# Two-block transformer kernel, second block's mixer: the norm of the differential heads moved two units later in VectorE's written order

## The chip, the core and the metric

One core of one Trainium2 chip runs the whole program. The metric is the device time of one execution in microseconds (us), the smaller the better; the time given for a kernel is the median over its runs. Two kernels are compared on the same chip.

## The reference, cut to what matters

The program computes two transformer blocks of two layers each over 256 tokens of width 1024, in float32. The change lies in the second block, in its `hybrid_mixer`, which runs once in each of the second block's two layers:

```python
def hybrid_mixer(n, pos, layer_idx, w_in, ...):
    proj = n @ w_in
    ...
    o_a = mla_causal_attention(q_a, k_a, v_a)                        # 6 latent heads, width 64
    o_b = diff_causal_attention(..., dvh, pos, slopes[:6], lam)      # 6 differential heads, width 64
    o_b = rmsnorm(o_b, sub_norm) * (1.0 - lam_init)                  # the norm that is moved
    o_c = moba_causal_attention(...)                                 # 4 block heads, width 64
    o = jnp.concatenate([from_heads(o_a), from_heads(o_b), from_heads(o_c)], axis=-1)
    return o @ w_out
```

After the mixer a layer has a cross attention to 256 memory tokens and a squared-relu feed-forward part.

## The kernel before, in words

The order of the work on each engine is written out by hand: one stream of instructions each for TensorE (PE), VectorE (DVE), ScalarE (ACT), GpSimd (POOL) and SyncE (SP, which issues the weight loads). Each stream runs in order, and the streams meet only in semaphores. Tokens lie on the 128 partitions in two tiles (t = 0, 1). A float32 product is made of three matmuls with rounded high and low parts (lines 937 to 939); ScalarE makes a weight piece's high part, VectorE its low part (`ahead`, line 2270).

The mixer's attention is cut into 12 **units**, here called unit 1 to unit 12 (in the code 0 to 11): 1 to 6 are differential heads, 7 and 8 the block heads, 9 to 12 the latent heads. Odd units are for token tile 0, even ones for tile 1. A unit passes through these steps:

- scores, TensorE (line 1090);
- **mask**, VectorE (`mask`, lines 2423 to 2433): adds the mask and finds each row's maximum;
- exponentials, ScalarE (line 1837);
- transposes of the probabilities, TensorE (line 1102), and their copy out, ScalarE (line 1851);
- **values**, TensorE (line 1145), all into one PSUM bank, so that the values of a unit wait until the unit before has been divided (`pe.wait_ge(o_out, u)`);
- **division**, VectorE (`end`: line 2457 the reciprocal, line 2465 the product, which writes the output rows H and signals `o_out`).

TensorE's order late in the stage is: scores of unit k+1, transposes of unit k-1, values of unit k-2, and so on. Between the transposes of unit 12 and the values of unit 11 stands its **tail**, `mixed` (line 1662): it waits for `rows_ready`, which the norm signals, and then transposes two batches of output heads (line 1009), the second of them the differential heads. Behind it come the values of units 11 and 12, one more batch, and then the output projection, whose first matmuls are at lines 937 to 939.

VectorE's loop in `attention` (line 2403) makes, in step i (counted from 0, units named from 1) for i above 7: the mask of unit i+1 (for i below 12), the division of unit i-2, then `between(i)`. In `between` the norm of the differential heads has two parts. In step 8 the squares, sums and the mean of the differential outputs are made, and POOL is asked for their power -1/2 (line 845). In step 10 VectorE waits for POOL, scales the factors by 1 - lambda (line 3116), and multiplies H by the factor and by the gain for both token tiles (lines 3119 and 3120, twice each): five instructions, the last of which signals `rows_ready`. In step 13, the last, it makes the low parts of the first two transposed batches (`turn_mix`).

Of the kernel before, what the change touches and what calls it, by code (L numbers as in the profile page):

```python
# [117 lines left out]
def build(nc, a, out):  # L118
    ctx = ExitStack()
    with ctx:  # L120
# [245 lines left out]
        def bc4(ap, n):  # L366

            return ap.unsqueeze(2).to_broadcast([ap.shape[0], ap.shape[1], n])
# [1878 lines left out]
        def _(dve):  # L2247
# [4 lines left out]
            def seq(ins):  # L2252

                done[0] += 1
                ins.then_inc(dve_seq, 1)
                dve.wait_ge(dve_seq, done[0])

            def power():

                c.pow += 1  # L2260
                dve.wait_ge(pow_out, c.pow)

            def ahead():

                limit = len(raw_of) if past_moe[0] else before_moe
                while c.split < min(c.piece + AHEAD, limit):
                    i = c.split
                    r, n = raw_of[i], size_of[i]
                    dve.wait_ge(w_hi, i + 1)
                    dve.tensor_tensor(Wl[:, i % SPLITS, 0:n], ring[:, r % RING, 0:n],  # L2270
                                      Wh[:, i % SPLITS, 0:n].bitcast(F32), ALU.subtract).then_inc(w_lo, 1)
                    c.split += 1
# [9 lines left out]
            def turn_mix(batches, batches_hi):  # L2282

                for (_, lo, _), (_, hi, _) in zip(batches, batches_hi):
                    c.mix += 1
                    dve.wait_ge(mix_hi, c.mix)
                    dve.tensor_tensor(lo, PS[:, c.turn % 4, :].rearrange("p (m s) -> p m s", m=2),
                                      hi.bitcast(F32), ALU.subtract).then_inc(turn_out, 1)
                    c.turn += 1
# [7 lines left out]
            def eps_in(n, width):  # L2297

                dve.tensor_scalar(st[:, 0:n], st[:, 0:n], 1.0 / width, EPS, ALU.mult, ALU.add).then_inc(pow_in, 1)
# [103 lines left out]
            def attention(units, extras={}, between=None, early={}, deep=None):  # L2403
# [66 lines left out]
                for i in range(count + 2):  # L2470
                    if i < count:
                        mask(i)
                    if i in early:
                        early[i]()
                    if deep is not None and i > deep + 1:
                        end(i - 3)
                    turned_values = units[0]["end"][0] == "nsa"
                    if turned_values and 1 <= i <= count:
                        weigh(i - 1)
                    if between is not None:  # L2480
                        between(i, count + 2)
                    if not turned_values and i >= 2 and (deep is None or i <= deep):
                        end(i - 2)
# [385 lines left out]
            for layer in range(LAYERS):  # L2869
# [170 lines left out]
                def second_glu():  # L3040

                    c.lin += 1
                    glu(1)

                attention(nsa_units(), nsa_extras, between, {1: second_glu})
                mix_low(1)
                ahead()
# [12 lines left out]
            for layer in range(LAYERS):  # L3060
# [42 lines left out]
                def between(i, n):  # L3103
                    if i in (0, 2, 5):
                        c.piece += 1
                        ahead()
                    elif i == 8:
                        for t in range(T):
                            view = H[:, t, 384:768]
                            seq(dve.tensor_tensor(norm_tmp[:], view, view, ALU.mult))  # L3110
                            seq(dve.tensor_reduce(st[:, 6 * t:6 * t + 6],
                                                  norm_tmp[:].rearrange("p (h d) -> p h d", d=64), AX, ALU.add))
                        eps_in(12, 64)
                    elif i == 10:
                        power()
                        seq(dve.tensor_scalar(rs[:, 0:12], rs[:, 0:12], 1.0 - lam0, None, ALU.mult))
                        for t in range(T):
                            view = H[:, t, 384:768].rearrange("p (h d) -> p h d", d=64)
                            seq(dve.tensor_tensor(view, view, bc4(rs[:, 6 * t:6 * t + 6], 64), ALU.mult))
                            ins = dve.tensor_tensor(view, view, bc[:, b0:b0 + 64].unsqueeze(1).to_broadcast([P, 6, 64]),  # L3120
                                                    ALU.mult)
                        ins.then_inc(rows_ready, 1)
                    elif i == n - 1:
                        turn_mix(t_mixed_lo[0:2], t_mixed[0:2])

                c.turn += len(t_latent(layer)) + len(t_diff)
                attention(mixer_units(layer), mix_extras, between, deep=DEEP)
                c.lin = base + 18
                turn_mix(t_mixed_lo[2:4], t_mixed[2:4])
# [83 lines left out]
```

## Time and profile before

| | |
|---|---|
| median of 3 runs | 2399.97 us (2398.38 to 2402.65) |
| the profiled execution, its own time | 2401.94 us |
| the profiled execution, its span | 2400.2 us |
| busy in the span: TensorE, VectorE, ScalarE, POOL | 2358.4, 1726.8, 1438.9, 69.7 us |
| instructions | 31905 |

The profile is of one execution. Its span is the time from the first to the last instruction; the execution's own time is 1.74 us longer. A row of the timeline gives the start, the length, the engine, the line, the operation, the tile written and the tiles read, and how many instructions were merged into the row; in square brackets stands how long the engine had been idle before, and which engine's work ended that. Starts and lengths overlap a little, since an engine takes up the next instruction before the last has fully ended. "PEclk" is the clock that was granted to TensorE, as a share of full speed.

### The profile page before, as it was taken

What the parts mean: (1) busy time and instruction counts of PE and PEld (TensorE: products, weight loads), DVE (VectorE), ACT (ScalarE), POOL (GpSimd) and SP (SyncE); (2) the same over time, 40 slices, a digit from 0 to 9 for tenths busy, and PEclk for the clock granted to TensorE, in tenths of its full rate; (3) what the DMA queues carried; (4) which work ended last, traced back from release to release, by engine and by line L of the source; (5) the groups of instructions that cost most, each with busy time, mean ns of one, the idle gap of its engine ahead of it and who ended that gap; (6) DMA issues with size and microseconds to landing.
All of it is one profiled execution on the core that took longest, in us unless ns stands there. A gap on an engine that the chain in (4) does not pass through costs nothing.

```text
span 2400.2 us, 31905 instructions
## 1 busy us (share of the span) xinstructions
PE 2358.4 (98%) x12092; PEld 1937.0 (81%) x12092; DVE 1726.8 (72%) x2123; ACT 1438.9 (60%) x1685; POOL 69.7 (3%) x79
## 2 busy tenths in 40 slices
PE   9999999999999999999999999999999999999998
PEld 8688888678888888888888888887788888787887
DVE  8665446759988889898988888767465565755555
ACT  6544445657777777777777777665544445554443
POOL 1000000001000000000000000001000000000000
PEclk9999999999999999999999999999999999999999
DMA  7545555419999999999999999615535542452551
GB/s 264 163 142 191 193 183 163 143 62 331 370 340 379 345 371 339 379 345 378 341 368 349 374 346 372 222 54 211 174 123 180 186 149 84 175 184 97 195 190 44
DMA packets 249704, 569.99 MB, mean 237 GB/s; under 512 B 9664, under 2 KB 20352, under 8 KB 249600
## 3 DMA queue, kind: packets, MB, share of 16 engines
q1 hardware_dynamic: 249456, 568.30, 67.3%
q8 instruction: 70, 1.15, 0.2%
q14 instruction: 34, 0.28, 0.0%
q10 hardware_dynamic: 144, 0.26, 0.0%
HBM read 562.82 MB, written 1.05 MB: 235 GB/s over the span
## 4 chain that ended last, share of the span: by engine, by line
PE 92%; DVE 5%; ACT 1%; issue 1%; POOL 0%; POOLq 0%; ACTq 0%; DVEq 0%
PE PS L937 27%; PE PS L939 26%; PE PS L938 26%; PE PS L1090 2%; PE PS L1564 1%; PE PS L1145 1%; PE PS L1393 1%; PE PS L1102 1%; PE PS L1213 1%; PE PS L1009 1%; PE PS L1128 1%; DVE Wl L2270 1%; PE PS L1034 1%; PE PS L1354 1%; PE PS L998 1%
## 5 line engine op out<-in xcount | busy, mean ns | idle before, releaser
L2706 DVE TENSOR_TENSOR Wl<-ring,Wh 128x2048 fp32r<-128x2048 f32 x334 | 761.9, 2298 | 100.9 <-ACT Wh L1988 100.9
L1988 ACT ACTIVATE Wh<-ring 128x2048 fp32r<-128x2048 f32 x334 | 639.8, 1918 | 127.8 <-PE PS L939 127.8
L2270 DVE TENSOR_TENSOR Wl<-ring,Wh 128x2048 fp32r<-128x2048 f32 (+2 forms) x192 | 431.2, 2251 | 278.0 <-ACT Wh L1743 277.4
L1743 ACT ACTIVATE Wh<-ring 128x2048 fp32r<-128x2048 f32 (+2 forms) x192 | 361.6, 1890 | 237.4 <-PE PS L939 236.6
L937 PE MATMUL PS<-Wh,HTh 128*128 128x512 f32 (+3 forms) x1184 | 465.8, 393 | 4.3 <-DVE Wl L2270 2.4
L939 PE MATMUL PS<-Wh,HTl 128*128 128x512 f32 (+3 forms) x1184 | 457.3, 386 | 0.0
L938 PE MATMUL PS<-Wl,HTh 128*128 128x512 f32 (+3 forms) x1184 | 456.7, 386 | 0.0
L937 PE MATMUL PS<-Wh,xgh 128*128 128x512 f32 x896 | 354.3, 395 | 1.8 <-DVE Wl L2706 1.2
L939 PE MATMUL PS<-Wh,xgl 128*128 128x512 f32 x896 | 349.5, 390 | 0.0
L938 PE MATMUL PS<-Wl,xgh 128*128 128x512 f32 x896 | 348.9, 389 | 0.0
L937 PEld LDWEIGHTS PS<-Wh,HTh 128*128 128x128 f32 x1184 | 223.5, 189 | 50.4 <-issue 4.2
L939 PEld LDWEIGHTS PS<-Wh,HTl 128*128 128x128 f32 x1184 | 223.4, 189 | 43.9
L938 PEld LDWEIGHTS PS<-Wl,HTh 128*128 128x128 f32 x1184 | 223.9, 189 | 41.1
L937 PEld LDWEIGHTS PS<-Wh,xgh 128*128 128x128 f32 x896 | 168.2, 188 | 37.5 <-DVE Wl L2706 2.0
L939 PEld LDWEIGHTS PS<-Wh,xgl 128*128 128x128 f32 x896 | 168.2, 188 | 35.9
L938 PEld LDWEIGHTS PS<-Wl,xgh 128*128 128x128 f32 x896 | 168.4, 188 | 33.5
L937 PE MATMUL PS<-Wh,hmh 128*128 128x512 f32 x448 | 175.9, 393 | 0.7 <-DVE hml L2720 0.7
L939 PE MATMUL PS<-Wh,hml 128*128 128x512 f32 x448 | 174.5, 389 | 0.0
L938 PE MATMUL PS<-Wl,hmh 128*128 128x512 f32 x448 | 174.3, 389 | 0.0
L937 PE MATMUL PS<-Wh,hTh 128*128 128x512 f32 x368 | 143.6, 390 | 0.0
L939 PE MATMUL PS<-Wh,hTl 128*128 128x512 f32 x368 | 143.2, 389 | 0.0
L938 PE MATMUL PS<-Wl,hTh 128*128 128x512 f32 x368 | 143.2, 389 | 0.0
(369 smaller groups left out, 2396.8 us busy)
## 6 DMA issues: line engine op xcount, KB each, us to landing
ring<-in_moe_w_gate SPq DMA_DIRECT2D x112, 1024.0 KB, 7.1
ring<-in_moe_w_up SPq DMA_DIRECT2D x112, 1024.0 KB, 7.3
ring<-in_moe_w_down SPq DMA_DIRECT2D x112, 1024.0 KB, 6.7
ring<-in_mlp_w SPq DMA_DIRECT2D x64, 1024.0 KB, 5.3
ring<-in_w_in SPq DMA_DIRECT2D x27, 1024.0 KB, 5.2
ring<-in_w_out SPq DMA_DIRECT2D x16, 1024.0 KB, 7.1
ring<-in_cross_wkv SPq DMA_DIRECT2D x16, 1024.0 KB, 12.4
ring<-in_ffn_w_gate SPq DMA_DIRECT2D x14, 1024.0 KB, 5.1
```

The source lines that it names most:

```text
L937: pe.matmul(out_, hi, high, start=start, stop=False)
L938: pe.matmul(out_, hi, low, start=False, stop=False)
L939: return pe.matmul(out_, lo, high, start=False, stop=stop)
L998: mm = pe.matmul(PS[:, bank, 0:n], lhs(kc, t), w[:, kc, c0:c0 + n], start=(kc == 0), stop=(kc == k - 1))
L1009: mm = pe.transpose(PS[0:width, c.turn % 4, off:off + rows], s, ident[0:rows, 0:rows])
L1034: mm = pe.transpose(PS[:, 2 * t + half, i * P:i * P + P], src[:, t, kc * P:kc * P + P], ident[:])
L1090: mm = pe.matmul(PS[:, 2 * (u % 2) + at[m] // 2, (at[m] % 2) * S:(at[m] % 2) * S + un["kl"]], q, key, start=(k == 0), stop=(k == len(un["s ...
L1102: mm = pe.transpose(PS[0:size, 4 + x % 2, m * P:m * P + P], un["home"][:, m, kb * P:kb * P + size], ident[:])
L1743: act.activation(Wh[:, i % SPLITS, 0:n], ring[:, r % RING, 0:n], ACT.Copy).then_inc(w_hi, 1)
L1988: act.activation(Wh[:, (base + i) % SPLITS, :], ring[:, (raw + i) % RING, :], ACT.Copy).then_inc(e_hi, 1)
L2270: dve.tensor_tensor(Wl[:, i % SPLITS, 0:n], ring[:, r % RING, 0:n], Wh[:, i % SPLITS, 0:n].bitcast(F32), ALU.subtract).then_inc(w_lo, 1)
L2706: dve.tensor_tensor(Wl[:, (base + i) % SPLITS, :], ring[:, (raw + i) % RING, :], Wh[:, (base + i) % SPLITS, :].bitcast(F32), ALU.subtract) ...
```

## The change

The second part of the norm is emitted in step 12 instead of step 10 of VectorE's loop. It is the same five instructions on the same data, and it applies to both layers. No other engine's order is touched. Step 10 then holds the mask of unit 11 and the division of unit 8; step 11 the mask of unit 12 and the division of unit 9; step 12 the division of unit 10 and then the norm; step 13 the division of unit 11 and `turn_mix`.

```diff
@@ -3111,7 +3111,7 @@
                             seq(dve.tensor_reduce(st[:, 6 * t:6 * t + 6],
                                                   norm_tmp[:].rearrange("p (h d) -> p h d", d=64), AX, ALU.add))
                         eps_in(12, 64)
-                    elif i == 10:
+                    elif i == 12:
                         power()
                         seq(dve.tensor_scalar(rs[:, 0:12], rs[:, 0:12], 1.0 - lam0, None, ALU.mult))
                         for t in range(T):
```

## Rows read from the trace of the kernel before

**Rows 1.** The page: the chain that ended last, by engine.
```profile
PE 92%; DVE 5%; ACT 1%; issue 1%; POOL 0%; POOLq 0%; ACTq 0%; DVEq 0%
```

**Rows 2.** The waits from 1624 to 1640 us (engine, line waited for: total us, times, longest).
```profile
DVE coef L2457 <- PE PS L1145: 4.8, 3, 2.2
...
PE PS L1145 <- DVE H L2465: 2.2, 3, 1.2
```

**Rows 3.** The timeline of VectorE, first of the two mixers (start, length).
```profile
1628.45 0.18 DVE L2457 RECIPROCAL coef<-PS 128x4 f32<-128x4 f32 x1 [1.54 <-PE PS L1145]
...
1629.01 0.16 DVE L3116 TENSOR_SCALAR rs<-rs 128x12 f32<-128x12 f32 x1
...
1630.86 0.56 DVE L3120 TENSOR_TENSOR H<-H,bc 128x384 f32<-128x384 f32 x1
1631.33 0.42 DVE L2423 CUSTOM_DVE_ANT_0 SM<-PS,causal 128x256 f32<-128x256 f32 x1
...
1632.21 0.18 DVE L2457 RECIPROCAL coef<-PS 128x4 f32<-128x4 f32 x1
1632.43 0.42 DVE L2465 TENSOR_TENSOR H<-PS,coef 128x256 f32<-128x256 f32 x1
1635.00 0.18 DVE L2457 RECIPROCAL coef<-PS 128x4 f32<-128x4 f32 x1 [2.15 <-PE PS L1145]
```

**Rows 4.** The timeline of TensorE, the same stretch.
```profile
1628.34 1.33 PE L1090 MATMUL PS<-scr 64*128 64x256 f32 x8
...
1630.54 1.00 PE L1145 MATMUL PS<-scr,PT 128*128 128x65 f32 x8
...
1633.00 1.97 PE L1145 MATMUL PS<-scr,PT 128*128 128x65 f32 x16 [1.23 <-DVE H L2465]
1634.80 0.61 PE L1102 MATMUL PS<-ident,SM 128*128 128x128 f32 x4
1635.25 1.04 PE L1009 MATMUL PS<-ident,H 128*128 128x128 f32 x8
...
1637.36 1.08 PE L1145 MATMUL PS<-scr,PT 128*128 128x65 f32 x8 [0.68 <-DVE H L2465]
...
1638.63 0.47 PE L937 MATMUL PS<-Wh,HTh 128*128 128x512 f32 x1
```

**Rows 5.** The timeline of POOL, the same stretch.
```profile
1624.19 2.26 POOL L845 TENSOR_TENSOR rs<-st,mhalf 128x12 f32<-128x12 f32 x1 [77.04 <-DVE st L2299]
```

**Rows 6.** The timeline of the second mixer: last gain of the norm, two TensorE rows.
```profile
2061.70 0.56 DVE L3120 TENSOR_TENSOR H<-H,bc 128x384 f32<-128x384 f32 x1
...
2063.84 1.97 PE L1145 MATMUL PS<-scr,PT 128*128 128x65 f32 x16 [1.23 <-DVE H L2465]
...
2066.09 1.04 PE L1009 MATMUL PS<-ident,H 128*128 128x128 f32 x8
```

**Rows 7.** Busy time by stretch, behind the first mixer.
```profile
core 0: us, PE busy (x) PEld busy (x) DVE busy (x) ACT busy (x) POOL busy (x), PEclk, DMA share, GB/s
1650.00:1700.00 50.00, 50.00 (x239) 41.73 (x238) 29.34 (x40) 26.28 (x34) 2.67 (x1) 1.00 0.75 259
```

**Rows 8.** The timeline of TensorE in the first block's attention, ahead of a clock fall.
```profile
115.81 0.61 PE L1102 MATMUL PS<-ident,SM 128*15 128x128 f32 x4 [1.52 <-DVE SM L2449]
```

**Rows 9.** Busy time by stretch: first block's attention, and the program's end.
```profile
117.00:118.00 1.00, 1.00 (x7) 1.00 (x8) 0.00 (x0) 0.04 (x1) 0.00 (x0) 0.59 0.05 16
...
2392.00:2396.00 4.00, 0.09 (x1) 0.00 (x0) 3.62 (x10) 1.15 (x1) 1.27 (x2) 1.00 0.32 129
```

**Rows 10.** The timeline of TensorE: a first-block projection (12 matmuls), then the mixer's own.
```profile
501.50 0.76 PE L937 MATMUL PS<-Wh,HTh 128*128 128x512 f32 x1 [0.46 <-DVE scr L3037]
...
506.32 0.40 PE L939 MATMUL PS<-Wh,HTl 128*128 128x512 f32 x1
...
1639.18 0.40 PE L939 MATMUL PS<-Wh,HTl 128*128 128x512 f32 x1
1639.41 0.40 PE L937 MATMUL PS<-Wh,HTh 128*128 128x512 f32 x1
```

## The prediction

> **What bounds the kernel now.** I read the page first. Its chain that ended last is 92% TensorE [rows 1], so the question for any edit is whether TensorE waits longer or shorter for it. I then took the waits around the first mixer's end. There TensorE stands still three times for a division on VectorE, 2.2 us in all, and VectorE in turn stands still three times for TensorE's values, 4.8 us [rows 2]. So the end of the mixer is a ping-pong of two engines, in which neither is full: values of a unit, its division, values of the next. What counts is which instructions of VectorE lie between the two.
>
> The timelines of the two engines give the order. VectorE divides unit 8 at 1628.45, and from 1629.01 to the end of the last gain at 1630.86 + 0.56 = 1631.42 it makes the norm; then come the mask of unit 12 from 1631.33 and the division of unit 9 from 1632.21 to 1632.43 + 0.42 = 1632.85 [rows 3]. TensorE had the values of unit 9 ready at 1630.54 + 1.00 = 1631.54, and waited 1.23 us until 1633.00 to start those of unit 10 [rows 4]. The reader should see that the norm delays this step: without it VectorE would have waited for TensorE at that point. POOL's power is done at 1626.45, long before the norm in either place [rows 5].
>
> The other thing to see is who waits for the norm. TensorE's tail, two batches of transposes at 1635.25, starts while the last transposes of unit 12 run out, with no idle time ahead of it [rows 4]. The norm was done 3.83 us before that. The change spends this slack.
>
> **The change, step by step, in the first mixer.** It takes five VectorE instructions with one signal and one wait for POOL from behind the division of unit 8, and puts them behind the division of unit 10. Nothing is added or removed, and there are no DMAs among them.
>
> Removed ahead of the mask of unit 12. The division of unit 8 to the norm's first instruction takes 1629.01 - 1628.45 = 0.56 us, so the mask could start at 1629.01, but its scores end at 1628.34 + 1.33 = 1629.67 [rows 4]. I take 0.03 us from TensorE's end to VectorE's start, as at 1633.00 + 1.97 to 1635.00 [rows 3, 4]: the mask starts at 1629.70 and ends 1632.21 - 1631.33 = 0.88 later, at 1630.58. VectorE now waits for the values of unit 9 and divides them from 1631.57. The division takes 0.64 us (1632.21 to 1632.85), TensorE's answer 0.15 us (1632.85 to 1633.00). So the values of unit 10 start at 1631.57 + 0.64 + 0.15 = 1632.36, which is **0.64 us earlier** than now. The mask's being early by 1.63 us is worth nothing more, because the transposes of unit 12 stand behind those values on TensorE.
>
> Added ahead of the tail. The values of unit 10 end at 1634.33 instead of 1634.97, and their division starts at 1634.36. The norm follows 0.56 us later, at 1634.92, and takes 1631.42 - 1629.01 = 2.41 us: it signals at 1637.33. The tail starts 0.15 us later, at 1637.48, where it now starts at 1635.25. That is **2.23 us later**. TensorE has the last transposes of unit 12 from 1634.16 to 1634.77 and then nothing: its stream is in order, and behind the waiting tail stand the values of units 11 and 12, which are otherwise ready. This is the new stall, 2.71 us long.
>
> Behind the tail nothing of the order changes. The values of unit 11 follow the tail, their division follows them and waits for nothing else, the values of unit 12 wait for that division as they do now (0.68 us), then the last batch and the projection, now at 1638.63 [rows 4]. ScalarE and the low parts made by VectorE follow the same transposes. All of it shifts by 2.23 us. The memory tokens' load is held until the values of unit 12, and shifts too; its users come later. Behind the mixer TensorE is busy 50.00 of 50 us [rows 7]: there is no wait of TensorE there that could take up the shift.
>
> The second mixer has the same pattern: last gain at 2061.70, values of unit 10 at 2063.84 after the same 1.23 us, tail at 2066.09 [rows 6]. The distances are 2.14 and 4.39 us, against 2.14 and 4.39 in the first. So it costs the same, and the **order alone costs 2 x 2.23 = 4.46 us**.
>
> **What the new gap does to TensorE's clock** is not in this sum, and the trace does not show such a gap at this place, so I bound it. Against any cost stands the program's end, where TensorE was busy for 0.09 of 4.00 us and its granted clock was still 1.00 [rows 9]. For a cost stands the first block's attention: after an idle stretch of 1.52 us at 115.81, with only short matmuls around it, the granted clock went from 1.00 to 0.59 in the microsecond from 117 [rows 8, 9], that is from the upper level of 2.4 GHz to the lower of 1.2 GHz for part of it. Our stage has gaps of 1.23 and 0.68 us now [rows 4]; it would have a gap of 2.71 us with short matmuls on both sides. A price for the fall comes from a projection run while the clock was low: its first 12 matmuls start from 501.50 to 506.32, 0.438 us apart, where the mixer's own projection has 0.23 [rows 10]. The 11 steps lose 11 x 0.21 = 2.3 us. The lower bound of a fall is 0, if it comes in the gap and is over before dense work starts; nothing in the rows makes a gain of it. Of these I take 1.2 us, half of 2.3, because part of the low stretch would pass while TensorE is idle in the gap or in short matmuls that also wait for divisions. I count one fall net of those that already happen: the runs of before lie 4.27 us apart, so they may hold one or two already, while the profiled one has none here.
>
> The Trainium skill ("TensorE: Matmul & The Clock Gate", section "A second HAM failure mode: psum-queue depth-cycling") says that frequent short idle times between groups of matmuls can make the clock swing between its levels, at a loss of throughput. By that rule the time is above the sum of the order alone; the fall at 117 agrees with it, the program's end does not speak for it.
>
> The sum: 4.46 + 1.2 = 5.7 us. Against the profiled execution's own time that is 2401.94 + 5.7 = 2407.6, which lies 1.97 us above the median of the runs; against the median, which I predict, 2399.97 + 5.7 = **2405.6 us**.
>
> **The rivals.**
> *The order alone* (0.35). The clock stays at 1.00 through the gap, as over the idle 4 us at the end. Then it is 2399.97 + 4.46 = 2404.4 us.
> *The clock falls in both mixers and for a full low stretch* (0.08): 4.46 + 2 x 2.3 = 9.1, so 2409.1 us.
> *The shift is taken up later* (0.10). For it: behind the mixer is a cross attention with waits of its own. Against it: those waits are on work that itself hangs on TensorE's order. If half of it is caught, 2402.2 us.
> *Not slower* (0.04). The two-engine ping-pong gains and the tail is not held: this needs the norm to be over before the last transposes of unit 12 end, at 1634.77. Then only the 0.64 us per mixer remains, 2399.97 - 1.3 = 2398.7 us. It would hold if VectorE had the norm's 2.41 us free between 1630.58 and 1634.36. It has idle time there, but the order puts the norm behind a division that starts only at 1634.36, so I see no way but a compiled order that differs from the written one. That the change does nothing is in the same case: the moved rows are on the chain today.
>
> **How the numbers follow.** The forecast, the order's cost and one fall of the clock more than before, has 0.43; its own range is 2404.8 (hardly any price of the fall) to 2408.5. The range for all reaches from 2402.8, under the case of the order alone, to 2409.0; outside it lie the not slower case, most of the case taken up later, and part of the double fall, under 2 in 10 together. About 0.2%, 4.8 us, is what a measurement of this kernel can tell from no change, and that is 2404.8: the order alone falls just under it. Slower by more: 0.43 of the forecast, 0.08, and a third of the 0.35, so 0.62. Faster by more than 0.2% no case gives: 0.01. The rest, 0.37, is within.
>
> **What would show it.** In the profile of the changed kernel the norm's first instruction (line 3116, now at 1629.01) comes some 5.9 us later, right behind a division; VectorE has a new wait of about 1 us for the values of unit 9; TensorE's wait ahead of the values of unit 10 falls from 1.23 to about 0.6 us; and a new wait of TensorE of 2.7 us appears at line 1009, released by H of line 3120, once in each mixer. From the mask of unit 11 to the first projection matmul there must be 2.2 us more at full clock. The granted clock by stretch decides between the forecast and the first rival: below 1.00 between the tail and some microseconds into the projection, or 1.00 throughout. I am wrong if the tail's wait is under 2 us, if TensorE has less idle time than before in the cross attention, or if the two mixers differ in anything but the clock.

## The result, and the profile after

| | kernel before | changed kernel |
|---|---|---|
| median | 2399.51 us (6 runs, 2394.4 to 2403.81) | 2412.64 us (6 runs, 2410.77 to 2413.95) |
| the profiled execution, its own time | 2401.94 us | 2412.96 us |
| its span | 2400.2 us | 2411.2 us |
| its mean granted clock | 0.994 | 0.991 |

The changed kernel is slower by a ratio of 1.0047, with an interval of 1.0035 to 1.0058. The ratio is worth 11.3 us; the medians of six runs each are 13.1 us apart, and the two profiled spans 11.0 us. The prediction has 5.7 us. The sign is right; the time lies 3.6 us above the range. Of the 90 runs of the kernel before that were made beside the experiments below, one, at 3387.45 us and a mean clock of 0.651, is left out throughout.

The page first: the instructions are 31905 as before, and the chain that ended last has the same split as in [rows 1].

```profile
PE 92%; DVE 5%; ACT 1%; issue 1%; POOL 0%; POOLq 0%; ACTq 0%; DVEq 0%
```

The waits from 1622 to 1650 us in the changed kernel (engine, line waited for: total us, times, longest):

```profile
PE PS L1009 <- DVE H L3120: 2.6, 1, 2.6
PE PS L1145 <- DVE H L2465: 1.5, 3, 0.7
```

The first row is new: TensorE's tail (line 1009) waits once, 2.6 us, for the last product of the norm. The last row was 2.2 us with 1.2 as the longest [rows 2]. So one wait became shorter and a new one came. VectorE's timeline in the first mixer says why:

```profile
1628.63 0.42 DVE L2423 CUSTOM_DVE_ANT_0 SM<-PS,causal 128x256 f32<-128x256 f32 x1 [0.63 <-PE PS L1090]
...
1630.49 0.18 DVE L2457 RECIPROCAL coef<-PS 128x4 f32<-128x4 f32 x1 [0.88 <-PE PS L1145]
...
1633.29 0.18 DVE L2457 RECIPROCAL coef<-PS 128x4 f32<-128x4 f32 x1 [2.15 <-PE PS L1145]
...
1633.85 0.17 DVE L3116 TENSOR_SCALAR rs<-rs 128x12 f32<-128x12 f32 x1
...
1635.70 0.56 DVE L3120 TENSOR_TENSOR H<-H,bc 128x384 f32<-128x384 f32 x1
```

The mask of unit 12 now waits 0.63 us for its scores, the division of unit 9 waits 0.88 us for its values, and the norm starts right behind the division of unit 10, at 1633.85. In [rows 3] the same instruction starts at 1629.01. TensorE's timeline, first mixer and then two rows of the second:

```profile
1628.52 1.09 PE L1102 MATMUL PS<-ident,SM_MIX 128*128 128x128 f32 x8
...
1631.28 1.97 PE L1145 MATMUL PS<-scr,PT 128*128 128x65 f32 x16 [0.60 <-DVE H L2465]
...
1636.31 1.97 PE L1009 MATMUL PS<-ident,H 128*128 128x128 f32 x8 [2.62 <-DVE H L3120]
1638.08 0.95 PE L1145 MATMUL PS<-scr,PT 128*128 128x65 f32 x4
1639.71 1.94 PE L1145 MATMUL PS<-scr,PT 128*128 128x65 f32 x8 [0.68 <-DVE H L2465]
1641.45 1.06 PE L1009 MATMUL PS<-ident,H 128*128 128x128 f32 x4
1642.16 0.78 PE L937 MATMUL PS<-Wh,HTh 128*128 128x512 f32 x1
...
1646.49 0.60 PE L1009 MATMUL PS<-ident,H 128*128 128x128 f32 x4
...
2073.33 1.97 PE L1009 MATMUL PS<-ident,H 128*128 128x128 f32 x8 [2.61 <-DVE H L3120]
...
2083.44 0.60 PE L1009 MATMUL PS<-ident,H 128*128 128x128 f32 x4
```

And the rows of the kernel before that these are compared with and that did not stand ahead of the prediction:

```profile
1629.61 1.09 PE L1102 MATMUL PS<-ident,SM_MIX 128*128 128x128 f32 x8
...
1636.12 0.56 PE L1145 MATMUL PS<-scr,PT 128*128 128x65 f32 x4
...
1638.27 0.61 PE L1009 MATMUL PS<-ident,H 128*128 128x128 f32 x4
1641.49 0.60 PE L1009 MATMUL PS<-ident,H 128*128 128x128 f32 x4
```

Read the lengths, not only the gap. The eight transposes of the tail took 1.04 us [rows 4] and now 1.97; the eight matmuls of the values of unit 12 took 1.08 and now 1.94. They are the same instructions at half speed. The windows of the changed kernel (columns as in [rows 7]) show it as the granted clock:

```profile
1630.00:1634.00 4.00, 3.09 (x27) 2.64 (x25) 1.29 (x5) 1.85 (x6) 0.00 (x0) 1.00 0.02 4
1634.00:1638.00 4.00, 1.69 (x8) 1.69 (x9) 2.15 (x5) 0.70 (x2) 0.00 (x0) 0.64 0.00 0
1638.00:1642.00 4.00, 3.32 (x17) 3.16 (x16) 1.93 (x6) 0.66 (x2) 0.00 (x0) 0.50 0.00 0
1642.00:1646.00 4.00, 4.00 (x13) 3.21 (x12) 0.88 (x2) 0.60 (x1) 0.00 (x0) 0.58 0.78 262
...
2068.00:2084.00 16.00, 12.40 (x61) 11.11 (x62) 5.79 (x15) 2.83 (x7) 0.00 (x0) 0.68 0.26 91
```

The clock goes from the upper level, 2.4 GHz (1.00), to the lower, 1.2 GHz (0.50), in the new gap, and stays low into the projection. Time at the lower level is the missing share of a window divided by one half: 0.36 x 4 / 0.5 = 2.9 us, then 4.0, then 0.42 x 4 / 0.5 = 3.4, together 10.2 us. The second mixer gives 0.32 x 16 / 0.5 = 10.2 us as well. In the profiled execution of before the clock is 1.00 in all of these stretches. The fall itself lies inside the gap, in a microsecond in which TensorE does nothing:

```profile
1635.00:1636.00 1.00, 0.00 (x0) 0.00 (x0) 0.97 (x3) 0.00 (x0) 0.00 (x0) 0.55 0.00 0
```

**Where the 11 us come from.** I measure the stage from the eight transposes of SM_MIX to the fourth batch of transposes (line 1009, x4), from start to start. Before it takes 1641.49 - 1629.61 = 11.88 us, after it 1646.49 - 1628.52 = 17.97 us: 6.09 us more. Between the starts of the tail and of the fourth batch nothing differs but the clock: 1641.49 - 1635.25 = 6.24 us before and 1646.49 - 1636.31 = 10.18 us after, so **3.94 us are the clock** and the other **2.15 us are the order** (predicted 2.23). The 3.94 split by starts of successive rows: tail 1.77 against 0.87, values of unit 11 with the wait 1.63 against 1.24, values of unit 12 1.74 against 0.91, last batch 0.71 against 0.36, the twelve projection matmuls 4.33 against 2.86. That is 0.90 + 0.39 + 0.83 + 0.35 + 1.47. More than half of it is in the short matmuls ahead of the projection. The second mixer gives 17.90 against 11.89 us, 6.01 more. The sum of both, 12.1 us, less the 1.09 us by which this execution was ahead when it reached the first mixer (1628.52 against 1629.61), is the 11.0 us of the span.

### The profile page after: what moved, and what is told of

Same layout as the page of the kernel before. It is cut to its first block, busy times and chain, and to the rows that moved or that the text cites. A ratio compares the mean times of both kernels' runs of the same rounds, so it can differ in the third digit from the quotient of the medians.

```text
span 2411.2 us, 31905 instructions
## 1 busy us (share of the span) xinstructions
PE 2365.9 (98%) x12092; PEld 1944.8 (81%) x12092; DVE 1726.5 (72%) x2123; ACT 1438.9 (60%) x1685; POOL 69.7 (3%) x79
## 4 chain that ended last, share of the span: by engine, by line
PE 92%; DVE 5%; ACT 1%; issue 1%; POOL 0%; POOLq 0%; ACTq 0%; DVEq 0%
PE PS L937 26%; PE PS L939 26%; PE PS L938 26%; PE PS L1090 2%; PE PS L1145 1%; PE PS L1564 1%; PE PS L1102 1%; PE PS L1393 1%; PE PS L1009 1%; PE PS L1213 1%; PE PS L1128 1%; DVE Wl L2270 1%; PE PS L1034 1%; PE PS L1354 1%; PE PS L998 1%
```

## The experiments

Two theories stood at this point. The first: the order costs what the prediction says, and all of the rest is the clock, which the gap brings down in both mixers. The rival: the low clock only goes along with a delay of another kind, so that it would stay if the clock did. Beside them stood the question whether the kernel before has falls of its own, which would change what counts as the price.

The kernel before was run again beside each group of kernels. Its medians were 2401.59 us beside e1 to e4, 2401.40 beside e5 to e8, and 2401.83 beside e9 to e12. Where an edit adds lines above, the same instruction stands one or two lines further down in the rows (L3121 or L3122 for L3120).

**e1: the norm one step later instead of two.** It is behind the division of unit 9.

```diff
-                    elif i == 10:
+                    elif i == 11:
```

> The norm's second part one step behind its old place, in step 11, behind the mask of unit 12 and the division of unit 9. Theory (each mixer loses first to the order, then to a fall of TensorE's clock in the new gap): here the norm ends before the last transposes of unit 12 do, so the tail waits for nothing or under 0.2 us, no gap over 1 us is there, the clock stays at 1.00 in both mixers, and each mixer is 0.6 us shorter than before: about 1.3 us off the kernel before, 0.9995 of it. Rival (any norm behind the last mask delays the mixer, because the divisions behind it come late): 1 to 4 us above the kernel before.

Measured: 2398.17 us median, ratio 0.9984 (0.9976 to 0.9993), so faster than before by 3.4 us, more than was expected. TensorE's timeline:

```profile
1629.52 1.09 PE L1102 MATMUL PS<-ident,SM_MIX 128*128 128x128 f32 x8
...
1632.28 1.97 PE L1145 MATMUL PS<-scr,PT 128*128 128x65 f32 x16 [0.60 <-DVE H L2465]
1634.08 0.61 PE L1102 MATMUL PS<-ident,SM 128*128 128x128 f32 x4
1634.53 1.07 PE L1009 MATMUL PS<-ident,H 128*128 128x128 f32 x8
...
1640.81 0.60 PE L1009 MATMUL PS<-ident,H 128*128 128x128 f32 x4
```

The wait ahead of the values of unit 10 is 0.60 us, as in the changed kernel, and the tail has no wait, as in before: it starts while the last transposes of unit 12 run out. The stage takes 11.29 us, 0.59 less than before (0.64 was worked out for this part). This is the gain of the change without its cost. It is 1.2 us for both mixers; the median gained 3.4, and the rest goes with the clock (below).

**e2 and e3: the gap filled, and the same filling in the kernel before.** The kernel has a helper, `unread`, whose 128x512 matmuls write to a PSUM bank that nobody reads. Ten of them go between the last transposes of unit 12 and the tail, the computed result being untouched. e2 is the change with them, e3 the kernel before with them.

```diff
-                def unread(i):
+                def unread(i, count=UNREAD):
...
-                    for k in range(UNREAD):
+                    for k in range(count):
...
+                amid[12, 1] = lambda: unread(12, 10)
```

> The change, and in each mixer ten 128x512 matmuls whose result nobody reads, between the transposes of unit 12 and the tail, where the changed kernel's TensorE stood idle for 2.62 us. Theory: they take 10 x 0.23 = 2.3 us and fit in the gap, the granted clock is 1.00 from 1630 to 1650 us, and only the cost of the order is left: 2 x 2.2 = 4.4 us above the kernel before (ratio 1.0018), some 8 us under the changed kernel. Rival (the loss of 12 us is in the waits themselves, the low clock only accompanies it): 11 to 13 us above the kernel before, as without them.

> The kernel before, with the same ten unread matmuls ahead of the tail in each mixer: TensorE is delayed there by 2.3 us, but busy. Theory: a delay of the tail of the same size as the change's, at full clock, costs its own length and no more: 2 x 2.3 = 4.6 us above the kernel before (1.0019), clock 1.00. Rival (whatever delays the tail costs about 6 us a mixer, since something behind it goes late): 11 to 13 us.

Measured: e2 2403.74 us, 1.0011 (1.0003 to 1.002); e3 2403.88 us, 1.0013 (1.0004 to 1.0022). TensorE's timeline of e2:

```profile
1626.49 1.09 PE L1102 MATMUL PS<-ident,SM_MIX 128*128 128x128 f32 x8
...
1631.42 2.56 PE L1672 MATMUL PS<-HTl 128*128 128x512 f32 x10
1634.28 1.09 PE L1009 MATMUL PS<-ident,H 128*128 128x128 f32 x8 [0.30 <-DVE H L3121]
...
1640.56 0.60 PE L1009 MATMUL PS<-ident,H 128*128 128x128 f32 x4
```

Its windows over both mixers:

```profile
1620.00:1650.00 30.00, 28.15 (x180) 23.69 (x179) 19.52 (x56) 13.20 (x23) 4.93 (x2) 1.00 0.39 142
2050.00:2085.00 35.00, 33.16 (x208) 26.98 (x208) 23.95 (x69) 17.47 (x32) 4.93 (x2) 1.00 0.39 142
```

This is the pair that decides. The ten matmuls are over before the norm is, since the tail still waits 0.30 us for it; so the tail is released by the same work as in the changed kernel, and what differs is the clock: 1.00 in both mixers. Its stage takes 1640.56 - 1626.49 = 14.07 us. Against the changed kernel's 17.97 that is **3.90 us for the clock**, against before's 11.88 it is **2.19 us for the order**. The rival falls, since the delay goes when the clock stays. With the extra work the change is at a ratio of 1.0011 to before, without it at 1.0047: 0.0036, or 8.6 us, are gained by adding work. In e3, where no gap is there to take them in, the same ten matmuls cost 14.17 - 11.88 = 2.29 us per mixer, and the clock is 1.00 too. The 1.23 us ahead of the values of unit 10 are still idle in e3.

**e4: the moved norm in the first of the two mixers only.**

```diff
-                    elif i == 10:
+                    elif i == (12 if layer == 0 else 10):
```

> The change in the first layer's mixer alone. Theory: the two mixers are alike and independent, each costs its order and its own clock fall: about 6 us above the kernel before (1.0025), the clock low from about 1635 to 1645 us and 1.00 in the second mixer. Rival (the first fall makes the second likelier, or the cost is not additive): under 4 or over 9 us.

Measured: 2405.65 us, 1.0015 (1.0006 to 1.0024), so the expected 1.0025 lies just above the interval. Its windows:

```profile
1620.00:1655.00 35.00, 30.84 (x186) 25.62 (x186) 20.53 (x71) 16.14 (x31) 3.98 (x2) 0.85 0.30 109
2050.00:2085.00 35.00, 32.58 (x239) 27.16 (x239) 25.35 (x90) 19.50 (x39) 2.76 (x2) 1.00 0.23 81
```

The clock falls in the mixer that has the gap and not in the one that has not. The missing 0.15 of 35 us is 10.5 us at the lower level, about as long as in the changed kernel. The stage of the first mixer takes 17.84 us, 5.96 more than before; the median is 4.1 more, over runs of before that hold falls of their own (e10, below). The fall in the first mixer did not bring one in the second; this is one execution's trace.

**e5: the kernel before, its own 1.23 us gap filled.** Four of the same matmuls stand in that gap, ahead of the values of unit 10 (`amid[11, 1] = lambda: unread(11, 4)`).

> The kernel before, with four unread 128x512 matmuls in each mixer in its own idle stretch of 1.23 us ahead of the values of unit 10 (4 x 0.23 = 0.9 us, so they delay nothing). Step 11 had come out 3.4 us under the kernel before, where the order explains 1.3. Theory (in some executions of the kernel before the clock falls in its mixers too, though not in the profiled one): the fillers keep it up, and the median is 1 to 3 us under the kernel before, 0.9988 to 0.9996, with fewer executions above 2402 us. Rival (the kernel before has no falls there, and the rest of step 11's gain lies elsewhere): the same as the kernel before within 0.0004.

Measured: 2399.42 us, 0.9992 (0.9982 to 1.0003). It is 2.0 us less by the medians, and the interval takes in no change. It alone does not settle whether the kernel before loses time to its own gap.

**e6: the norm cut in two.** Its scaling and the first token tile are in step 11, the second tile and the signal in step 12.

```diff
-                    elif i == 10:
-                        power()
-                        seq(dve.tensor_scalar(rs[:, 0:12], rs[:, 0:12], 1.0 - lam0, None, ALU.mult))
-                        for t in range(T):
+                    elif i in (11, 12):
+                        if i == 11:
+                            power()
+                            seq(dve.tensor_scalar(rs[:, 0:12], rs[:, 0:12], 1.0 - lam0, None, ALU.mult))
+                        for t in (i - 11,):
...
-                        ins.then_inc(rows_ready, 1)
+                        if i == 12:
+                            ins.then_inc(rows_ready, 1)
```

> The scaling of the factors and the norm of token tile 0 in step 11, token tile 1 alone (two instructions, 1.15 us) and the signal in step 12. By the order the tail starts 1.15 - 2.41 = 1.26 us earlier than in the changed kernel, 1.0 us later than in the kernel before, after a gap of about 1.4 us: 2 x 1.0 = 2 us. Theory (a fall hangs on how long and how sparse the stretch is): with a gap of 1.4 us the clock falls in some executions or none, so 2 to 5 us above the kernel before (1.0008 to 1.002). Rival (any wait of the tail brings the clock down): 9 to 10 us above, 1.004.

Measured: 2405.45 us, 1.0019 (1.001 to 1.0028), inside the expected 2 to 5 us. TensorE's timeline and the windows:

```profile
1633.18 1.93 PE L1009 MATMUL PS<-ident,H 128*128 128x128 f32 x8 [1.35 <-DVE H L3121]
...
2067.88 1.09 PE L1009 MATMUL PS<-ident,H 128*128 128x128 f32 x8 [1.35 <-DVE H L3121]
...
2070.04 1.83 PE L1145 MATMUL PS<-scr,PT 128*128 128x65 f32 x8 [0.68 <-DVE H L2465]
```

```profile
1620.00:1650.00 30.00, 27.11 (x162) 23.37 (x163) 17.94 (x55) 12.78 (x22) 4.93 (x2) 0.89 0.36 129
2050.00:2085.00 35.00, 32.11 (x205) 26.76 (x204) 23.94 (x73) 16.38 (x32) 4.93 (x2) 0.95 0.35 129
```

With half the gap the clock still falls in both mixers, but the low stretch is shorter and not at the same place in the two mixers. In the first it takes in the tail: 0.11 x 30 / 0.5 = 6.6 us. In the second the tail runs at full speed (1.09 us) and the clock is down only at the values of unit 12, behind one more wait of 0.68 us: 0.05 x 35 / 0.5 = 3.5 us. The same gap behind the same work costs different amounts, by when the fall comes, and the fall need not come in the gap.

**e7: the change with three matmuls in the gap instead of ten** (`unread(12, 3)`).

> The change, with only three unread matmuls in the gap (0.7 of its 2.6 us), the number the program itself puts into its stage at two earlier places. Theory: the idle rest is 1.9 us, less than what brought the clock down in every timed run and profile of the change, more than what the kernel before has; the fall comes in part of the executions, 5 to 9 us above the kernel before (1.002 to 1.0038), with a wide spread. Rival (the fall needs a gap over 2 us): 4.4 us above, as with ten. Rival (three do nothing): 12 us.

Measured: 2408.2 us, 1.003 (1.002 to 1.0041), which is between e2 and the changed kernel, and 6.8 us over before where 5 to 9 were expected. TensorE's timeline and the windows:

```profile
1634.13 0.94 PE L1672 MATMUL PS<-HTl 128*128 128x512 f32 x3
1636.99 1.09 PE L1009 MATMUL PS<-ident,H 128*128 128x128 f32 x8 [1.92 <-DVE H L3121]
```

```profile
1620.00:1650.00 30.00, 26.55 (x163) 21.56 (x164) 16.31 (x55) 13.41 (x30) 2.27 (x1) 0.89 0.26 96
2050.00:2085.00 35.00, 31.54 (x222) 26.12 (x221) 22.17 (x78) 16.80 (x37) 2.27 (x1) 0.95 0.20 73
```

The idle time falls from 2.62 to 1.92 us, the low stretches become shorter (6.6 and 3.5 us), and the falls stay. In both mixers they come later than in the changed kernel: the tail still runs at full speed (1.09 us), and the clock goes down at 1639.0 and 2075.8, at the next wait. Three matmuls take a part of the loss away, ten take all of it.

**e8: e1 with two matmuls in its remaining gap** (`unread(11, 2)`), to see whether a still fuller stage is better.

> Step 11, and two unread matmuls in each mixer in the idle 0.60 us ahead of the values of unit 10 (0.45 us). Theory: step 11 leaves no stretch sparse enough for a fall, so they change nothing: 0.9984 of the kernel before, as without them, within 0.0006. Rival (the clock still falls in some executions of step 11): 1 to 2 us under step 11, 0.998 of the kernel before.

Measured: 2398.88 us, 0.9994 (0.998 to 1.0008). The centre missed the expected 0.9984 by 0.0010, and the interval takes in both that and no change: it shows no gain over e1, and cannot show a loss.

**e9: the changed kernel with TensorE's tail behind the values of unit 11 instead of ahead of them.** Those values wait for nothing that the norm makes, so they fill a part of the gap with useful work. `deep` is given for the mixer alone.

```diff
-                        if i == n and tail:
+                        if i == n and tail and deep is None:
                             tail[1](u0 + tail[0])
                         if i >= 2:
                             values(i - 2)
+                        if i == n and tail and deep is not None:
+                            tail[1](u0 + tail[0])
```

> The change, with TensorE's tail behind the values of unit 11 instead of ahead of them. By the order: the values of unit 11 run while VectorE makes the norm, their division follows the norm at once, and the values of unit 12 stand directly behind the tail instead of 0.68 us after another division. The tail starts as late as in the changed kernel, but the projection 1.2 us earlier: 1.0 us a mixer over the kernel before instead of 2.2. TensorE still has some 2 us idle ahead of the tail. Theory (order and clock add up): the clock falls in both mixers in nearly all executions, as in the change, so 8 to 10 us over the kernel before, and 2 us at equal mean clock. Rival (what stood behind the waiting tail was the loss): 2 us or less over the kernel before, with the clock up.

Measured: 2406.45 us, 1.0019 (1.0007 to 1.0031), so 4.6 us over before where 8 to 10 were expected. TensorE's timeline and the windows:

```profile
1636.46 1.09 PE L1009 MATMUL PS<-ident,H 128*128 128x128 f32 x8 [1.61 <-DVE H L3122]
...
2068.93 1.97 PE L1009 MATMUL PS<-ident,H 128*128 128x128 f32 x8 [1.60 <-DVE H L3122]
```

```profile
1620.00:1650.00 30.00, 26.76 (x177) 21.88 (x176) 20.01 (x59) 14.59 (x28) 4.93 (x2) 1.00 0.36 130
2050.00:2085.00 35.00, 32.15 (x198) 26.79 (x197) 22.64 (x72) 16.14 (x31) 4.93 (x2) 0.90 0.34 122
```

In one execution, after the same work and the same gap of 1.6 us, the clock held at 1.00 in the first mixer and fell in the second, for 0.10 x 35 / 0.5 = 7.0 us. I had counted on two full falls; whether such a gap brings the clock down is not certain each time. The order came out at 1.53 us a mixer instead of 1.0 (the stage of the first mixer takes 1642.07 - 1628.66 = 13.41 us): the projection's first matmul has a new wait of 0.38 us there, for a low part that VectorE makes (line 2289).

**e10 and e11: two more executions of the kernel before with their traces.** Nothing is edited.

> The kernel before again, for another profile. Theory: where the mean clock of the span is 0.994 or more, the granted clock is 1.00 in both mixers; where it is 0.993 or less, one of the mixers shows a low stretch behind its idle 1.23 us. Rival: its low stretches are all in the first block's attention and at the end, and differ only in length.

> A second look at the kernel before. Theory: at a mean clock of 0.993 or less one mixer shows a low stretch behind its idle 1.23 us, at 0.994 or more none does. Rival: all its low stretches are in the first block and at the end.

Measured: e10 has 2400.25 us at a mean clock of 0.995, e11 2399.02 us at 0.996. In e11 both mixers are at 1.00. In e10 the second is at 1.00 and the first is not, which the expectation had excluded. Its windows and two rows of its TensorE timeline:

```profile
1628.00:1632.00 4.00, 2.77 (x22) 2.56 (x22) 1.53 (x9) 1.20 (x4) 0.00 (x0) 0.90 0.00 0
1632.00:1636.00 4.00, 3.32 (x19) 3.21 (x18) 1.45 (x5) 1.96 (x4) 0.00 (x0) 0.67 0.00 0
```

```profile
1629.63 2.21 PE L1145 MATMUL PS<-scr,PT 128*128 128x65 f32 x16 [1.23 <-DVE H L2465]
...
1632.50 1.91 PE L1009 MATMUL PS<-ident,H 128*128 128x128 f32 x8
```

So the clock of the kernel before does fall in its own mixer, 1.6 us after its gap of 1.23 us has ended, but not in each execution, and briefly: 0.8 + 2.6 = 3.4 us, over before the projection. The stage takes 13.54 us there, 1.66 more than the 11.88 of the profile of before.

**e12: e1 once more, on another chip.**

> Step 11 once more, on another chip if it comes to one, to see whether it beats the kernel before by the order alone or by more. Theory: 1.3 us by the order in every execution, and in those executions in which the kernel before loses its clock in a mixer (a mean granted clock of 0.993 or less) some 2 to 4 us more: 0.9984 to 0.9995, and no execution of step 11 at 0.993 or less. Rival (the first result was the luck of few runs): 0.9995 to 1.0005, with mean clocks spread as those of the kernel before.

Measured: 2398.96 us, 0.999 (0.9979 to 1.0001). The centre agrees with e1 to within its interval, though this interval ends just above no change.

**All runs against their mean granted clock.** Each run of a kernel lists it. Over 89 runs of the kernel before on three chips:

| mean granted clock | runs | time, us |
|---|---|---|
| 0.992 | 4 | 2405.88 to 2407.09 |
| 0.993 | 13 | mean 2404.6 |
| 0.994 | 29 | mean 2402.4 |
| 0.995 | 17 | mean 2399.7 |
| 0.996 | 19 | mean 2399.4 |
| 0.998 and 0.999 | 7 | mean 2394.1 |

The order of the program is the same in all, so these 13 us are not the order's. A line of one slope (and a level of its own for each kernel) through the runs of all kernels gives 1.83 us for 0.001 of mean clock and leaves a deviation of 0.8 us for a single run. Where two kernels' runs are compared at the same mean clock, the difference should be their order alone, which the stages at full clock, or the rows around the tail, give apart from it:

| kernel | by the stages, both mixers | at equal mean clock | mean clock of its runs |
|---|---|---|---|
| changed | 2 x 2.15 = +4.3 us | +4.2 us | 0.9908 |
| e1, e12 | 2 x -0.59 = -1.2 | -1.7, -1.4 | 0.9956, 0.9952 |
| e2 | 2 x 2.19 = +4.4 | +4.5 | 0.9957 |
| e3 | 2 x 2.29 = +4.6 | +4.8 | 0.9959 |
| e4 | 2.15 (one mixer) | +1.8 | 0.9931 |
| e5 | 2 x 0 = 0 | -0.3 | 0.9953 |
| e6 | 2 x 0.89 = +1.8 | +2.2 | 0.9933 |
| e7 | 2 x 2.15 = +4.3 | +4.5 | 0.9931 |
| e8 | 2 x -0.61 = -1.2 | -1.6 | 0.9956 |
| e9 | 2 x (13.41 - 11.88) = +3.1 | +2.1 | 0.9932 |

The kernel before has 0.9947. For the changed kernel 0.0039 less clock is 7.2 us by the slope, and with the order's 4.2 us that makes 11.4 us, as the ratio has it (11.3); the two mixers give 2 x 3.9 = 7.8 for the same term. The last row fits worst, by 1.0 us, and that is more than a mean of 12 runs should stray where a single run strays by 0.8: one price for all low time is only roughly right.

The same list counts how often a kernel fell. Runs with a mean clock of 0.993 or less: before 17 of 89; the kernels with a shorter gap than before (e1, e12), with matmuls in it (e2, e5, e8), or with matmuls behind it (e3) 0 of 70; e4 9 of 11, e6 7 of 11, e7 6 of 8, e9 10 of 12; the changed kernel 6 of 6. So the low runs go with idle time in the mixer that is neither short nor filled. This fits e1 too: part of its 3.4 us would be that it no longer has the runs with a fall that before has, since its gap there is 0.60 instead of 1.23 us. That is argued from these counts; no trace pair shows it.

## Why the prediction was wrong, point by point

**Right: the chain.** TensorE bounded the kernel before and after, at 92% of the chain.

**Right: the part removed ahead of the mask of unit 12.** VectorE's waits of 0.63 us for the scores and 0.88 us for the values of unit 9 (about 1 was said), and TensorE's wait of 0.60 us instead of 1.23, are in the rows. e1 is this part alone, with the stage 0.59 us shorter against 0.64.

**Right: the part added ahead of the tail.** The tail's wait is 2.62 and 2.61 us, against 2.71 predicted, released by line 3120, once in each mixer. The order's cost is 2.15 us by the rows and 2.19 us by e2, against 2.23.

**Right: nothing takes up the shift.** TensorE is busy for all 50 us from 1650 in the changed kernel too, and the differences of the two mixers, 6.09 and 6.01 us, arrive whole in the span. That the two mixers differ in nothing held as well.

**Wrong: "Of these I take 1.2 us, half of 2.3", under "What the new gap does to TensorE's clock".** This term of the sum was mis-sized, in two ways that multiply. The number of falls was taken as one more than before; the changed kernel has a fall in each mixer of its profile, and all six of its runs are at 0.990 to 0.992. And the price of a fall was taken from a projection alone and then halved, because the rest of the low stretch would pass in the gap and in short matmuls that wait anyway. The runs show 3.9 us per fall. The argument of the short matmuls was the wrong way round: tail, values of unit 11, values of unit 12 and last batch are one chain with the divisions, each of them lengthens at the lower clock, and each wait behind them keeps its length (0.68 us in both kernels). They lose 2.47 us, and the projection, 1.47 us, is the smaller part. The full 2.3 was itself the price of only 4.8 us at the lower level. The trace of before has whole low stretches, with a granted clock of 0.51 over 117 to 131 us and of 0.53 over 496 to 507, so 13.7 and 10.3 us long; the new ones are 10.2. So the term is 7.8 instead of 1.2 us, and 4.4 + 7.8 = 12.2 us stand against 5.7. The 11.3 measured are a little less; they are counted from runs of before, of which some seem to hold falls themselves.

**The rivals.** *The clock falls in both mixers and for a full low stretch* was the mechanism that came, at a chance of 0.08 and priced at 9.1 us, also too low, for its 2 x 2.3 again counted the projection only. *The order alone*, the likeliest rival at 0.35, is what e2 shows by its stage, and would have needed the gap filled; its ground, a clock that stays at 1.00 over the idle end of the program, was a misreading (next point). *The shift is taken up later* and *Not slower* have nothing in the rows for them; e1 is what the latter describes, at the place in the order where the norm is in fact over in time.

**What should have tipped it.** The two rows on the clock were weighed as one against the other. But the window at the program's end [rows 9] stops too early. The one behind it, and the same place in e10, where the last matmul ends at 2390.4, read:

```profile
2396.00:2400.00 4.00, 0.00 (x0) 0.00 (x0) 0.75 (x1) 0.72 (x1) 0.20 (x1) 0.66 0.36 133
```

```profile
2392.00:2396.00 4.00, 0.00 (x0) 0.00 (x0) 2.77 (x7) 0.94 (x2) 0.93 (x1) 0.55 0.32 131
```

So the clock falls in the idle end as well, some 5 us after the last matmul in the profile of before and 2.0 us after it in e10. The end of the program is no evidence against a fall; it shows that the time until one varies. And the fall at 117 [rows 8, 9] comes after an idle time of 1.52 us amid short matmuls, which is the new stage's own pattern with a smaller gap. The Trainium skill ("TensorE: Matmul & The Clock Gate", section "A second HAM failure mode: psum-queue depth-cycling") says that frequent short idle times between groups of matmuls can make the clock swing, at a loss of throughput. The runs agree, with 17.97 us against 14.07 for a stage that differs only in whether the gap is filled. The same page (section "Terms") puts the penalty of a low stretch at its length times the share of the clock that is missing, which for 10.2 us would be 5.1 us, an estimate by that page. The rows show 3.9, since part of the low stretch passes in the gap (some 1.2 us, from the fall to the tail) and in the wait of 0.68 us; here the measurement decides.

**What stays open.** How long a gap must be, and behind what work, is not settled. With a longest gap of 1.23 us the clock fell in one mixer of e10 and in none of e11; with 1.35 us in both mixers of e6; with 1.6 us in one mixer of e9 and not in the other. Nor is it settled that the longest gap counts: each of these stages has waits of 0.3 to 0.7 us beside it, some falls come behind the gap (e7, e10, the second mixer of e6), and no run held the sum of the waits fixed while the longest one changed. That low runs of before come from its mixer in general is supported by the counts above but shown by a trace only in e10; falls in the first block's attention, like that at 117 [rows 9], may have their part in them. The cost of e9 is 1 us less at equal clock than its stage says, and why was not found. Nor was it tried whether the runs of before at 0.998 and above lack every fall.

## What to carry to other kernels

Two engines that hand work back and forth leave slack at one end of a chain and a wait at the other; a block of work moved across several handovers should go just far enough that the wait is gone and the slack is not yet used up. Here one step later gains 0.16% (e1) or 0.10% (e12, whose interval just takes in no change), of which the order is 0.05%, and two steps later lose 0.47%. A new idle time of TensorE of one or two microseconds on the critical path is to be priced at its own length plus a possible fall of the clock, and that price is taken over all matmuls on the path until the clock is back, short ones included; the fall in each mixer cost more here (3.9 us) than the delay that brought it (2.2 us). To tell the two apart, fill the gap with matmuls whose result nobody reads, few enough to end before the wait does, and see in the trace that the clock held: whatever goes away then was the clock.

## What the runs showed of the hardware that was not expected

In a stage of short matmuls whose longest idle gap was only 1.35 us the granted clock went from 1.00 to 0.50 in both mixers of e6, and ten 128x512 matmuls that compute nothing in a gap of 2.6 us kept it at 1.00 (e2), where three shortened the low stretch but did not prevent it (e7). Behind dense work too an idle time of 2.0 us was enough once, at the end of e10.

The spread of one unchanged kernel, 2394 to 2407 us over 89 runs, follows the mean granted clock at some 1.8 us for 0.001. Most of what looks like noise in this kernel goes with the clock, so comparing runs at equal mean clock tells small changes of the order apart that medians of a few runs don't: e2's order costs 4.5 us at equal clock, while its median is only 2.2 us above that of before.
